# The gates' arithmetic of an mLSTM layer, moved from a stage of its own into the front projections' stage

## The reference, cut to what matters

```python
q, k, v, o, gates = jnp.split(h @ w_in, [hqk, 2 * hqk, 2 * hqk + hv, 2 * hqk + 2 * hv], axis=-1)
gates = gates.astype(f32) + b_gates.astype(f32)
log_i = gates[..., :A_HEADS]
log_f = jax.nn.log_sigmoid(gates[..., A_HEADS:])
# per chunk of tokens, carry (C, n, m):
b = jnp.cumsum(lf, axis=1)
d = b[:, :, None, :] - b[:, None, :, :] + li[:, None, :, :]
a = b + m[:, None, :]
m_t = jnp.maximum(a, d.max(axis=2))          # running maximum
inter = jnp.exp(a - m_t)
m_new = jnp.maximum(b_end + m, g.max(axis=1))
```

## Time and profile before

| | us |
|---|---|
| median of 3 runs | 2780.44 (2778.39 to 2782.85) |
| the profiled execution | 2775.34 |
| its span, first to last instruction | 2773.7 |
| TensorE busy | 2342.2 (84%) |
| VectorE busy | 1395.3 (50%) |
| ScalarE busy | 1034.6 (37%) |
| mean granted TensorE clock | 0.906 of full |

### The profile page before, as it was taken

How to read it: one execution, slowest core, us unless ns; L and a number is a source line. 1 busy time by engine, 2 the same in 40 slices (tenths; PEclk the granted TensorE clock), 3 DMA queues, 4 the chain that set the end, 5 groups by cost and what they waited for, 6 DMA issues and landing times. The chain is left out here.

```text
span 2773.7 us, 40230 instructions
## 1 busy us (share of the span) xinstructions
PE 2342.2 (84%) x11749; PEld 1764.8 (64%) x11749; DVE 1395.3 (50%) x2315; ACT 1034.6 (37%) x1732; POOL 343.0 (12%) x403
## 2 busy tenths in 40 slices
PE   2999997596968999999598999999989589999940
PEld 0876664464856778788376755666568477788730
DVE  2411111555876655756384243333358767655738
ACT  1211121343123654645242333343341246654623
POOL 0000000253001000100010224100000011101115
PEclk7899998577978999999898899999999789999975
DMA  6156562554235876876544445322241368866944
GB/s 254 49 197 215 203 204 85 141 157 160 92 119 174 294 248 227 291 269 237 192 147 152 137 149 169 115 87 96 95 164 56 113 233 299 292 241 225 335 156 147
DMA packets 193498, 500.40 MB, mean 180 GB/s; under 512 B 19347, under 2 KB 39284, under 8 KB 186901
## 3 DMA queue, kind: packets, MB, share of 16 engines
q1 hardware_dynamic: 164804, 403.80, 43.0%
q0 software_dynamic: 19056, 66.20, 6.9%
q10 hardware_dynamic: 9536, 29.13, 2.8%
HBM read 433.45 MB, written 68.77 MB: 181 GB/s over the span
## 5 line engine op out<-in xcount | busy, mean ns | idle before, releaser
L1771 DVE TENSOR_TENSOR e_wl<-e_raw,e_wh 128x1024 fp32r<-128x1024 f32 x384 | 449.3, 1219 | 97.3 <-ACT e_wh L1682 97.0
L1682 ACT CAST e_wh<-e_raw 128x1024 fp32r<-128x1024 f32 x384 | 382.1, 1048 | 96.0 <-DMA e_raw<-in_e_up 38.8
L1601 PE MATMUL e_psG<-e_wh,e_xh 128*128 128x512 f32 x784 | 321.7, 410 | 10.2 <-issue 7.4
L1603 PE MATMUL e_psG<-e_wh,e_xl 128*128 128x512 f32 x784 | 311.9, 398 | 0.0
L1602 PE MATMUL e_psG<-e_wl,e_xh 128*128 128x512 f32 x784 | 310.3, 396 | 0.0
L1601 PE MATMUL e_psY<-e_wh,e_hh 128*128 128x512 f32 x392 | 159.2, 406 | 22.6 <-DVE e_hl L1794 22.6
L313 PE MATMUL in_ps<-in_w_upper,in_h_upper 128*128 128x512 f32 (+1 forms) x432 | 177.2, 410 | 0.0
L1601 PEld LDWEIGHTS e_psG<-e_wh,e_xh 128*128 128x128 f32 x784 | 148.9, 190 | 42.6 <-issue 8.3
L209 DVE TENSOR_TENSOR in_w_lower<-in_w_raw,in_w_upper 128x512 f32 (+1 forms) x48 | 33.2, 693 | 282.5 <-ACT in_w_upper L203 282.2
L1603 PEld LDWEIGHTS e_psG<-e_wh,e_xl 128*128 128x128 f32 x784 | 148.4, 189 | 37.0
L314 PE MATMUL in_ps<-in_w_lower,in_h_upper 128*128 128x512 f32 (+1 forms) x432 | 171.6, 397 | 0.0
(11 more groups left out here) (519 smaller groups left out, 4389.4 us busy)
## 6 DMA issues: line engine op xcount, KB each, us to landing
e_raw<-in_e_gate SPq DMA_DIRECT2D x32, 2048.0 KB
e_raw<-in_e_up SPq DMA_DIRECT2D x32, 2048.0 KB, 8.4
e_raw<-in_e_down SPq DMA_DIRECT2D x32, 2048.0 KB, 7.7
x<-in_ada_w SPq DMA_DIRECT2D x40, 1024.0 KB, 5.5
yrows<-e_y ACTq DMA_DIRECT2D x49, 512.0 KB, 7.9
x<-in_cache SPq DMA_DIRECT2D x64, 320.0 KB, 3.4
a_pages<-in_cache SPq DMA_DIRECT2D x64, 320.0 KB, 3.5
in_w_raw<-in_a_w_in POOLq DMA_DIRECT2D x48, 256.0 KB, 4.6
```

The costliest lines, as they stand in the source:

```text
L1601: T.matmul(out, upper[:, k, :], wh[:, z, cols], start=k == 0, stop=False)
L1603: mm = T.matmul(out, lower[:, k, :], wh[:, z, cols], start=False, stop=k == PIECES * n - 1)
L1682: S.copy(wh[:, z, c * PC:(c + 1) * PC], raw[:, z, c * PC:(c + 1) * PC]).then_inc(s_hi[z], 1)
L1771: V.tensor_tensor(wl[:, z, at], raw[:, z, at], wh[:, z, at].bitcast(F32), ALU.subtract).then_inc(s_lo[z], 1)
```

## The change

`stage_gates` is gone. Its instructions are in `stage_front`'s lists, with these differences. VectorE's pieces of chunks 2 to 5 are written out one by one, with the gates' parts between them. TensorE has four insertions, after tiles (1,3), (1,7), (2,2) and (4,3), written as (chunk, tile). ScalarE has Exp after (1,0), Ln after (1,1) and the exponentials after (3,7). SyncE loads bias and m at the very start, and stores M, m and the factor in chunk 5. The gates' tiles lie in `g.x[6:9]` and in the place of shift and scale, which are free after chunk 0. The accumulator banks are those of the turned h and of the gate products. So `stage_out_proj` must reload all of x: tiles 4 to 7 instead of 4 and 5, and the sample. The drains around semaphores are fewer, and exp(-b - M) is one VectorE operation in place of two.

```diff
@@ stage_front, SyncE
             sp.dma_start(cT[:], g.cT).then_inc(s_c, 16)
+            sp.dma_start(bg[:], g.a_b_gates.broadcast_to([P, GATES])).then_inc(s_gb, 16)
+            sp.dma_start(mprev[:, PT:NC], g.state_mT).then_inc(s_gb, 16)
             load_bias(sp, 0)
...
+                    if c == CHUNKS - 1 and t == 1:
+                        sp.wait_ge(s_args, 1)
+                        sp.dma_start(g.m_out, mout[:]).then_inc(s_gst, 16)
+                        spread(g.MD, M)
+                        sp.wait_ge(s_exps, 1)
+                        spread(g.interD, e3[0])
@@ stage_front, VectorE
-            for c in range(2, CHUNKS):
-                with v.Fori(0, KD // 2) as i:
-                    for par in range(2):
-                        lower(v, c, i, par)
-                group_out(c - 1)
+            def exponents():
+                V.tensor_copy(sixteen[:, 3, :, :], uh[:, SEQ:N].rearrange("h (a b) -> h a b", b=16))
+                v.drain()
+                for part, (lo, n) in enumerate(((0, P), (PT, CS))):
+                    V.tensor_tensor(chunks(e3[0])[part], before(part), chunks(M)[part], ALU.subtract)
+                    V.tensor_tensor(chunks(e3[2])[part], chunks(uh)[part],
+                                    mend[:, lo:lo + PT].unsqueeze(2).broadcast_to([H, PT, n]), ALU.subtract)
+                V.scalar_tensor_tensor(out=e3[1][:], in0=bh[:], scalar=-1.0, in1=M[:], op0=ALU.mult, op1=ALU.subtract)
+                V.tensor_tensor(dec[:], mprev[:], mend[:], ALU.subtract)
+                v.drain()
+                v.sem_inc(s_args, 1)
...
+            gate_parts()
+            piece(2, 0)
+            gate_log()
+            piece(2, 1)
+            gate_logf()
+            for k in range(2, 5):
+                piece(2, k)
+            sums_out()
+            for k in range(5, KD):
+                piece(2, k)
+            group_out(1)
+            piece(3, 0)
+            turned_out()
+            for k in range(1, 4):
+                piece(3, k)
+            sample_out()
+            piece(3, 4)
+            running_max(ca, cb, 1)
...
+            piece(4, 4)
+            chunk_ends()
+            piece(4, 5)
+            maxima()
+            piece(4, 6)
+            exponents()
+            piece(4, 7)
+            group_out(3)
+            piece(5, 0)
+            spread_out()
+            for k in range(1, 5):
+                piece(5, k)
+            factors_out()
+            for k in range(5, KD):
+                piece(5, k)
+            group_out(4)
@@ stage_front, TensorE
+            def turn_back():
+                pe.wait_ge(s_dd, 1)
+                for x in range(3):
+                    o = x * TILES * H
+                    for t in range(PT):
+                        T.transpose(psG[:, 0, o + t * H:o + (t + 1) * H], e3[x][:, t * P:(t + 1) * P], g.ident[0:H, 0:H])
+                    T.transpose(psG[:, 0, o + PT * H:o + TILES * H], wide[:, x, :], g.ident[0:H, 0:H])
+                T.transpose(psG[:, 0, 3 * TILES * H:3 * TILES * H + H], wide[:, 3, :], g.ident[0:H, 0:H])
+                T.matmul(psG[:, 1, 0:H * NC], g.ones[0:H, :], decd[:], start=True, stop=True).then_inc(s_back, 1)
...
                     job(c, c % 2, t)
+                    if (c, t) == (1, 3):
+                        gate_sums()
+                    if (c, t) == (1, 7):
+                        turn_gates()
+                    if (c, t) == (2, 2):
+                        turn_sample()
+                    if (c, t) == (4, 3):
+                        turn_back()
@@ stage_front, ScalarE
+                    if (c, t) == (1, 0):
+                        act.wait_ge(s_gabs, 1)
+                        nc.scalar.activation(gabs[:], gabs[:], ACT.Exp).then_inc(s_le, 1)
+                    if (c, t) == (1, 1):
+                        act.wait_ge(s_gabs, 2)
+                        nc.scalar.activation(gabs[:], gabs[:], ACT.Ln).then_inc(s_ln, 1)
+                    if (c, t) == (3, 7):
+                        act.wait_ge(s_args, 1)
+                        for e in e3:
+                            nc.scalar.activation(e[:], e[:], ACT.Exp)
+                        nc.scalar.activation(dec[:], dec[:], ACT.Exp).then_inc(s_exps, 1)
@@ stage_gates: removed
@@ stage_out_proj
-        PARTS = ((0, 1), (1, 4), (4, x_tiles))
+        PARTS = ((0, 1), (1, 4), (4, PT))
...
-            if x_tiles == PT:
-                sp.dma_start(g.x[0:NSAMP, PT, :], x_kept[SEQ:N, :]).then_inc(s_again[2], 16)
+            sp.dma_start(g.x[0:NSAMP, PT, :], x_sample).then_inc(s_again[2], 16)
```

More of the change, by code:

```diff
@@ new lines, in turned_out, with sample_out, running_max @@
+            def turned_out():
+                v.wait_ge(s_tu, 1)
+                V.tensor_copy(uh[:, 0:SEQ], turned)
+                V.tensor_copy(bh[:, 0:SEQ], sums).then_inc(s_ub, 1)
+            def sample_out():
+                v.wait_ge(s_ts, 1)
+                V.tensor_copy(uh[:, SEQ:N], turned[:, 0:NSAMP])
+                V.tensor_copy(bh[:, SEQ:N], turned[:, NSAMP:2 * NSAMP])
+                v.drain()
+                V.tensor_copy(ca[:], uh[:])
+                v.drain()
+            def running_max(src, dst, k):
+                for part, n in zip(range(2), (P, CS)):
+                    a, d = chunks(src)[part], chunks(dst)[part]
+                    if k < n:
+                        V.tensor_tensor(d[:, :, k:n], a[:, :, k:n], a[:, :, 0:n - k], ALU.max)
+                        V.tensor_copy(d[:, :, 0:k], a[:, :, 0:k])
+                    else:
+                        V.tensor_copy(d, a)
+                v.drain()
@@ new lines, in chunk_ends @@
+            def chunk_ends():
+                for part, (lo, n) in enumerate(((0, P), (PT, CS))):
+                    V.tensor_copy(mend[:, lo:lo + PT], chunks(cb)[part][:, :, n - 1])
+                    V.tensor_copy(bend[:, lo:lo + PT], chunks(bh)[part][:, :, n - 1])
+                V.memset(mprev[:, 0:1], 0.0)
+                v.drain()
+                for c in range(PT):
+                    V.tensor_tensor(mend[:, c:c + 1], mend[:, c:c + 1], mprev[:, c:c + 1], ALU.max)
+                    v.drain()
+                    nxt = mprev[:, c + 1:c + 2] if c + 1 < PT else mout[:, 0:1]
+                    V.tensor_tensor(nxt, mend[:, c:c + 1], bend[:, c:c + 1], ALU.add)
+                    v.drain()
+                V.tensor_tensor(mend[:, PT:NC], mend[:, PT:NC], mprev[:, PT:NC], ALU.max)
+                v.drain()
+                V.tensor_tensor(mout[:, 1:1 + BATCHES], mend[:, PT:NC], bend[:, PT:NC], ALU.add)
+                v.drain()
@@ new lines, in before, with maxima @@
+            def before(part):
+                lo, n = ((0, P), (PT, CS))[part]
+                return mprev[:, lo:lo + PT].unsqueeze(2).broadcast_to([H, PT, n])
+            def maxima():
+                for part in range(2):
+                    V.tensor_tensor(chunks(M)[part], chunks(cb)[part], before(part), ALU.max)
+                V.memset(wide[:], 1.0)
+                v.drain()
+            def exponents():
+                V.tensor_copy(sixteen[:, 3, :, :], uh[:, SEQ:N].rearrange("h (a b) -> h a b", b=16))
+                v.drain()
+                for part, (lo, n) in enumerate(((0, P), (PT, CS))):
+                    V.tensor_tensor(chunks(e3[0])[part], before(part), chunks(M)[part], ALU.subtract)
[3 more added lines that the diff above has]
+                V.tensor_tensor(dec[:], mprev[:], mend[:], ALU.subtract)
+                v.drain()
+                v.sem_inc(s_args, 1)
@@ new lines, in _ @@
+            sample_out()
+            piece(3, 4)
+            running_max(ca, cb, 1)
+            piece(3, 5)
+            running_max(cb, ca, 2)
+            piece(3, 6)
+            running_max(ca, cb, 4)
+            piece(3, 7)
+            group_out(2)
+            piece(4, 0)
+            running_max(cb, ca, 8)
+            piece(4, 1)
+            running_max(ca, cb, 16)
+            piece(4, 2)
+            running_max(cb, ca, 32)
+            piece(4, 3)
+            running_max(ca, cb, 64)
@@ new lines, in _ @@
+                if c not in (1, 3):
+                    tiles(act, rest)
+                    continue
+                for t in range(TILES):
+                    rest(t, t // 2, t % 2 if t < PT else 2, rows_of(t))
+                    if (c, t) == (1, 0):
[9 more added lines that the diff above has]
+                        nc.scalar.activation(dec[:], dec[:], ACT.Exp).then_inc(s_exps, 1)
@@ L3415, in build, with gsb @@
         g.slots_used = sb("slots_used", [P, 1], I32)
-        with nc.sbuf_tensor("gates", [P, TILES, GATES], F32) as g.gates:
+        with ExitStack() as gated:
+            def gsb(n, s):
+                return gated.enter_context(nc.sbuf_tensor(n, s, F32))
+            g.gates = gsb("gates", [P, TILES, GATES])
+            g.u = gsb("u", [P, TILES, H])
+            g.factors = gsb("factors", [P, 3, TILES, H])
+            g.decay = gsb("decay", [P, PAIRS, PT])
```

(1 more changed line is left out.)

305 lines of the change are left out of this document (99 added, 206 removed).

## The result

The changed kernel takes 2743.58 us (median of 4 runs, 2741.13 to 2753.92), the kernel before, timed beside it, 2781.64 us: a ratio of 0.987, interval 0.9842 to 0.9898. The forecast was 2744 us and faster. So 38 us of the 45.7 us of the removed stage have arrived, or 28 to 44 by the interval.

The account below looks back on a forecast made before the run. TensorE alone was taken to bound the front, with the gates stage wholly on the path: -45.7 + 8.3 + 0.4 + 0.6 = -36.4 us, applied to the median 2780.4 for 2744.0 us, range 2734 to 2755.

Parts of the forecast that it names:

- TensorE's term: Gates' matmuls inserted among the front's own, counted in full: 8.3 us added, ends 5.8 and 16.7.
- The sums and the turn: Front, TensorE: running sums by two f32 matmuls, 0.6 us; 18 transposes into 8 partitions and for the sample, 1.9 us.
- The turn back: Front, TensorE: 28 transposes back and one two-pass matmul, paced by weight loads at 0.11 us each, 3.3 us.
- getting back into the long products: Front, TensorE: returning to 512-column products after each of four insertions, 0.25 us each, 1.0 us.
- The clock fall: Front, TensorE: one fall of the clock at the turn back, 1.5 us; none at the lower end, four at the upper.
- What hides under TensorE: Front: the gates' VectorE, ScalarE and SyncE work fits within tile times of 6.64 us, so no piece is late.
- The start: Two loads issued before the modulation weights delay the front by between 0 and 0.8 us, taken as 0.4.
- The table load: mLSTM stage: its first Exp needs a table load of 1.28 us in front; cost 0.6 us, ends 0 and 1.3.
- The reload: Output projection: reloading four tiles and the sample instead of two is hidden, 0 us, upper end 3.4.
- The clock gift in the mLSTM stage: Rival: full clock holds or returns early in the stage's first 25 us, -8 us, 2736 us; chance 0.12.
- Late rounding: Rival: front pieces rounded late delay four chunks by 2 us each, 8 us, 2752 us; chance 0.08.
- The fall for the rest of the front: Rival: clock falls at the turn back and stays at half, 69 us over 14 tiles, 2813 us; chance 0.02.

Follow-up runs that it names:

- the first profile: The changed kernel, unaltered, in its first profiled execution: span 2741.6 us, 32.1 us less than that of the kernel before.
- the second: The changed kernel, unaltered, profiled and timed again: 2745.92 us, ratio 0.9846 to the kernel before.
- experiment 4: The changed kernel with the transposes back made four times over in one run (84 more): 2752.32 us, ratio 0.9874 to the kernel before.
- experiment 3: The changed kernel with VectorE's gates work in one lump between pieces 6 and 7 of chunk 4: 2758.38 us, ratio 0.9894 to the kernel before.
- second pair: The kernel before and the changed kernel, both unaltered, each profiled and timed again: 2784.71 us (ratio 0.9997) and 2745.92 us (0.9846).
- experiments 1 and 7: The changed kernel unaltered again, 2745.92 us (ratio 0.9846), and with an early Exp of 8 columns in the mLSTM stage, 2740.49 us (0.9846).
- before's second profile: The kernel before, unaltered, profiled again and timed against itself: 2784.71 against 2782.95 us, ratio 0.9997; profiled span 2787.8 us.

## Why the prediction was right

**The bound and the removed stage: right.** TensorE had no idle time in the front, and the stage behind it went as a whole. Predicted 45.7 us; measured 45.5, as the gap from last matmul to first load fell from 51.16 to 5.64 us. It was said that these two would be 5 to 6 us apart.

**TensorE's term: its total was high, and so were nearly all its parts.** Predicted 8.3 us, measured 4.4 in the first profile and 304.19 - 298.22 = 6.0 in the second. (With before's front chunks 1 to 5 take 297.8 to 298.3 us in four profiles.)
- The sums and the turn were predicted at 0.6 and 1.9 us and took 0.47 and 1.83 (without the sample's two).
- The turn back was predicted at 3.3 us, from the step "weight loads set the pace at either clock". That step failed. Its row was the front's gate products, 128 features wide in fp32r, which follow each other by 0.11 us at full clock. The 8-partition f32 transposes, which had about the same distance at half clock (0.107), go at 0.062 us at full clock: 2.16 us for all.
- The 1.0 us for getting back into the long products is not there: 0.47 + 1.83 + 2.16 and the sample's two transposes at 0.20 are 4.66, already more than the 4.41 us.
- The clock fall of 1.5 us was right in kind and size, 1.6 us, but it came in only two of four executions with the transposes in one run, and the first profile is one of those without. It was only argued by its likeness to the gate products; experiment 4 shows it, with a longer run of the same transposes at whose end the clock is at half.

**What hides under TensorE: right, and shown.** VectorE's parts fitted, and experiment 3 gives the other side: the same work in one lump costs 14 us. VectorE's busy time between 200 and 450 us rose from 29.7 to 52.1 us, by 22 and not by the 30 that were named. The prediction put the exponents at 4.4 us (4.15 measured) and ScalarE's exponentials at 4.9 (4.5 measured, 335.94 to 340.45).

**The small terms.** The start: 0.4 us predicted, not seen. Chunk 1 began at 159.25 to 161.72 us in five profiles with the two loads ahead and at 159.92 to 163.66 in four of before's front; a term of this size is below that scatter. The table load: 0.6 us predicted, 0.3 to 1.2 where it was the last to come. The Trainium skill's drain of some 1380 ns behind a table load ("ScalarE: Activation LUTs", section "What ACT_TABLE_LOAD costs") does not appear here either: load at 475.61, Exp at 476.90. The reload: 0 predicted and 0 in the output projection, in both kernels.

**The total.** By the profiles the local sum is -42.4 (first) and -43.5 us (second pair) against the predicted -37.0 for it, and the mLSTM's table load gives back up to 1.2. Timed: -38.1, then by the ratios of experiments 1 and 7 about -43 (36 to 50). So 2744.0 against 2743.6 is closer than the working deserved, and that is luck: the local sum was 5.4 us too small, and the timed difference of the first runs was smaller than the local one. The intervals of the three ratios overlap, and no run shows whether that was scatter or something given back behind the boundary. The two local sums hold the start as well, which scatters by some 4 us. Without it the change is worth 45.5 - 4.4 = 41.1 us, or 39.5 where the clock fell, against 45.7 - 8.3 = 37.4 predicted. Of the 5.4 us, TensorE's term is 3.9 (1.5 for a fall that this execution did not have, 1.1 for the turn back, 1.0 for the way back into the long products, the rest in the sums and the turn), the start is 1.7 (0.4 late predicted, 1.3 early seen, which is scatter), and the boundary takes 0.2 off.

**The rivals.** The clock gift in the mLSTM stage did not come: the stage took 142.4 and 137.4 us against 141.7 and 137.4, and over all ten profiles 137.4 to 141.7 with before's front and 137.4 to 143.0 with the gates in it. What the rival built on, 25 us at half clock, was one execution's. Over 25 us from about the stage's first transposes on, before's second profile has a mean of 0.77 and the changed kernel's first one 0.70; these are the two rows.

```profile
516.30:541.30 25.00, 16.93 (x114) 13.88 (x115) 8.07 (x31) 14.94 (x39) 8.16 (x9) 0.77 1.10 288
...
472.50:497.50 25.00, 18.81 (x133) 14.76 (x133) 8.06 (x31) 15.30 (x39) 6.88 (x7) 0.70 1.09 296
```

At its start the stage is at half clock, as the prediction's reason against had it (0.50 between 469 and 475). Late rounding did not happen, and needs a lump to happen. The fall for the rest of the front did not happen: even 6.3 us of small work at half clock (370.8 to 377.1 in experiment 4) were followed by full clock from about 381.

## What to carry to other kernels

A stage of small operations that hop between engines costs its whole length; spread out under a stage that one engine bounds, it costs only what it adds to that engine, here 4 to 6 us of 45. What makes it free is that each part fits in the time between two deadlines of the host stage: find the deadlines (here one weight piece per tile, hard only at the chunk's end), and cut the work to them. Price what goes onto the bounding engine by a row of the same form at the clock it will run at, and expect the clock to fall in a long run of small matmuls, as it did in experiment 4; that a shorter run avoids it is not shown.

## What the runs showed of the hardware that was not expected

- Transposes of 8 x 128 f32 follow each other by 0.062 us at 2.4 GHz and by 0.107 at 1.2 GHz, while gate products of 128 x 128 fp32r with 16 moving columns take 0.11 us each at 2.4 GHz.
- A run of 28 such transposes and a small product (2.2 us) was followed by a fall to 1.2 GHz in two executions and by none in two. In experiment 4 the clock fell while the run was going on, 3.5 us after its start, and was at 2.4 GHz again some 2 us after the 512-column products of the next tile had begun.
- Two profiles of the kernel before differ by 14 us in all, although the longer one's mLSTM stage was the shorter by 4.3 us (137.4 against 141.7), while each kernel's front stays within 3.6 us up to the boundary. A change of 40 us is safe against that; a difference of two single profiles in a later stage is not.
